# The MLP's down product as seven half-size block products, with the weights' block sums made by ScalarE and adding transfers

## The reference

```python
h2 = rms_norm(x, norm_mlp[layer])
x = x + jnp.square(jax.nn.relu(h2 @ w_ff1[layer])) @ w_ff2[layer]
return rms_norm(x, norm_final)
```

## Time and profile before

| | |
|---|---|
| Time, median of 3 runs | 1755.04 us (1754.81 to 1755.32) |
| The profiled execution's own time | 1756.95 us |
| Its span, first to last instruction | 1755.4 us |
| PE busy | 1741.1 us |
| DVE busy | 801.4 us |
| ACT busy | 587.6 us |
| POOL busy | 80.9 us |

### The profile page before, as it was taken

One profiled execution on the slowest core, in us unless ns is written; L12 is line 12 of the kernel. 1 busy time (PEld: TensorE's weight loads), 2 busy tenths in 40 slices (PEclk: granted clock), 3 DMA queues, 4 the chain that ended last, 5 costly groups with the idle time before them and its releaser, 6 DMA issues.

```text
span 1755.4 us, 21872 instructions
## 1 busy us (share of the span) xinstructions
PE 1741.1 (99%) x8476; PEld 1276.0 (73%) x8476; DVE 801.4 (46%) x1160; ACT 587.6 (33%) x753; POOL 80.9 (5%) x148
## 2 busy tenths in 40 slices
PE   8999999999999999999999999999999999999998
PEld 7888888874444444454788877788888888888886
DVE  6323338453242424333673455656675544324423
ACT  5334433332211212122454533444532253113313
POOL 3000000000000000000020022200000000000000
PEclk9999999999999999999999999999999999999999
DMA  6222222858999999999313221222242222222222
GB/s 207 94 97 94 72 72 97 340 213 347 422 422 422 422 421 422 422 422 413 109 50 125 96 89 56 73 97 96 96 173 99 101 96 96 96 96 96 96 97 82
DMA packets 91169, 326.34 MB, mean 186 GB/s; under 512 B 8720, under 2 KB 9248, under 8 KB 66528
## 3 DMA queue, kind: packets, MB, share of 16 engines
q1 hardware_dynamic: 89328, 320.18, 48.0%
q0 software_dynamic: 1776, 5.26, 0.9%
HBM read 319.13 MB, written 6.29 MB: 185 GB/s over the span
## 4 chain that ended last, share of the span: by engine, by line
PE 98%; DVE 1%; ACT 0%; DMA 0%; issue 0%; SPq 0%; DVEq 0%; ACTq 0%
PE bank L2321 62%; PE bank L2652 13%; PE bank L2665 6%; PE bank L2560 3%; PE bank L2607 3%; PE bank L2346 3%; PE bank L2894 2%; PE bank L2832 1%; PE bank L2776 1%; PE bank L2853 1%; PE bank L2534 0%; PE bank L2925 0%; PE bank L2523 0%; DMA w_stage<-in_w_in 0%; PE bank L2931 0%; PE bank L2910 0%
## 5 line engine op out<-in xcount | busy, mean ns | idle before, releaser
L2321 PE MATMUL bank<-act_hi,w_hi 128*128 128x512 f32 x992 | 389.7, 393 | 0.0
L2321 PE MATMUL bank<-act_hi,w_lo 128*128 128x512 f32 x992 | 386.3, 389 | 0.0
L2321 PE MATMUL bank<-act_lo,w_hi 128*128 128x512 f32 x992 | 386.2, 389 | 0.0
L1460 DVE TENSOR_TENSOR w_lo<-w_stage,w_hi 128x2048 fp32r<-128x2048 f32 x98 | 224.4, 2289 | 348.9 <-ACT w_hi L859 348.8
L859 ACT ACTIVATE w_hi<-w_stage 128x2048 fp32r<-128x2048 f32 x98 | 187.8, 1917 | 387.7 <-PE bank L2321 382.0
L2652 PE MATMUL bank<-ring,xgT 128*64 128x512 f32 x992 | 215.7, 592 | 0.2 <-ACT xgT L1078 0.2
L2321 PEld LDWEIGHTS bank<-act_hi,w_hi 128*128 128x128 f32 x992 | 186.3, 188 | 40.1 <-issue 2.5
L2321 PEld LDWEIGHTS bank<-act_hi,w_lo 128*128 128x128 f32 x992 | 186.2, 188 | 39.1
L2321 PEld LDWEIGHTS bank<-act_lo,w_hi 128*128 128x128 f32 x992 | 186.4, 188 | 37.5
L2652 PEld LDWEIGHTS bank<-ring,xgT 128*64 128x64 f32 x992 | 70.7, 137 | 141.5 <-issue 141.0
L2665 PE MATMUL bank<-ring,gatedT 128*64 128x512 f32 x512 | 113.4, 595 | 0.0
(11 more groups left out here) (429 smaller groups left out, 2036.1 us busy)
## 6 DMA issues: line engine op xcount, KB each, us to landing
ring<-in_w SPq DMA_DIRECT2D x188, 1024.0 KB, 12.0
w_stage<-in_w_in SPq DMA_DIRECT2D x45, 1024.0 KB, 5.1
w_stage<-in_w_ff SPq DMA_DIRECT2D x32, 1024.0 KB, 5.2
w_stage<-in_w_out SPq DMA_DIRECT2D x8, 1024.0 KB, 5.1
extra<-in_w SPq DMA_DIRECT2D x4, 1024.0 KB, 8.2
branch_gates<-gate_out POOLq DMA_DIRECT2D x16, 256.0 KB, 2.5
w_stage<-in_w_proj_gla SPq DMA_DIRECT2D x4, 1024.0 KB, 10.0
w_stage<-in_w_pg SPq DMA_DIRECT2D x3, 1024.0 KB, 5.1
```

The costliest lines, as they stand in the source:

```text
L1460: dve.tensor_tensor(w_lo[s][:, 0:ktiles, :], w_stage[s][:, 0:ktiles, :], w_hi[s][:, 0:ktiles, :].bitcast(F32), ALU.subtract).then_inc(w_lo ...
L2321: ins = pe.matmul(gb[j][:, :], left, right, start=(kc == 0 and k == 0 and n_pass == 0), stop=(kc == g.chunks - 1 and k == g.ktiles - 1 and ...
```

## The change

With the hidden tile as a 2 x 2 block matrix (token halves by hidden-feature halves, each block 256 x 1024) and the half's weights likewise (1024 x 512 blocks B11, B12, B21, B22), the eight block products of the down product become seven, each of one operand of the list `part_operand` with one weight operand: B11, B21, T2 = B22 - B12 + B11, T1 = B12 - B11, T3 = B22 - B12, B22, and B21 - T2. Part `n` has two steps `v = 2n, 2n+1`, each with one 1 MB weight operand, and serves 2 token tiles only: 24 matmuls a step. Parts that share a bank pair are left to add up in it (`part_first`), and each part is followed by an addition of its two banks to one quarter of `x` (`add_part`).

- `hid_hi`, `hid_lo` and `relu_sq` are gone. DVE squares straight into `hidden`, and each part's operand is split when its turn comes (`part_split_hi` on ACT, `part_split_lo` on DVE, 128x2048 each). `relu_t` has two buffers in place of four.
- The operands' sums are four DVE subtractions or additions of 128x2048 in each half (`sum_three`, `sum_two`, `sum_one`, `sum_four`).
- The weights' sums are made in SBUF: ACT negates a tile of 128x2048 (`negate`, eight in each half), and POOL then issues a DMA from `w_ff2` in DRAM with `accum_op=ALU.add` into that tile (`add_block`: in each half nine of 1 MB or, for `t3_late`, two of 512 KB in place of one, in one fixed order). Waits on POOL's queue keep the adds of one `kc` in order.
- The loops over the MLP's units on ACT and DVE are written out. The ends of the rows are taken in another order at the very end (token tiles 0 and 1 are done after part 5; tiles 2 and 3 after part 6). Elsewhere, three semaphores are merged with others, with the same waits.

```diff
-        last = Gemm(up, 2, FH // 512, "dve")
+        last = Gemm(up, 2, PARTS, "dve", tiles=PARTS)
...
-        hid_hi = at("hid_hi", F + 0, [P, FH // P, T], F32R)
-        hid_lo = at("hid_lo", F + 16, [P, FH // P, T], F32R)
-        relu_t = [at(f"relu_t{s}", F + 32 + s, [P, T]) for s in range(4)]
-        relu_sq = [at(f"relu_sq{s}", F + 36 + s, [P, T]) for s in range(4)]
+        hidden = at("hidden", F + 0, [P, FH // P, T])
+        a11, a12, a21, a22 = (hidden[:, 8 * i:8 * i + 8, 256 * q:256 * q + 256] for q in range(2) for i in range(2))
+        t3_late = a11.rearrange("p (k c) n -> p k c n", c=2)
+        part_hi = [at(f"part_hi{s}", F + 16 + 8 * s, [P, 8, 256], F32R) for s in range(2)]
+        part_lo = [at(f"part_lo{s}", F + 20 + 8 * s, [P, 8, 256], F32R) for s in range(2)]
+        b_one = [at(f"b_one{s}", F + 36 - 4 * s, [P, 4, 512]) for s in range(2)]
+        s_two = at("s_two", F + 36, [P, 8, 256])
+        b_sum = [at(f"b_sum{s}", F + 40 + 4 * s, [P, 4, 512]) for s in range(2)]
+        relu_t = [at(f"relu_t{s}", F + 48 + s, [P, T]) for s in range(2)]
...
+        part_bank = [(gb[0:2], mb[0:2], gb[0:2], gb[2:4], gb[0:2], gb[2:4], gb[0:2])[n] for n in range(PARTS)]
+        part_first = (True, True, False, True, False, False, False)
+        part_quarter = ((0, 0), (0, 0), (0, 1), (1, 1), (1, 1), (0, 1), (1, 0))
+        bank_before = (None, None, 0, None, 2, 3, 4)
+        S3, S2, S1, S4 = 1, 2, 3, 4
+        SUM_LOADS, STAGE_LOADS, ONE_LOADS, ADDS, NEGATED = 1, (2, 1), (3, 3), (5, 6), 8
+        step_stage = (w_stage[0], w_stage[1], w_stage[0], b_one[1], b_sum[0], b_sum[1], w_stage[0], w_stage[1],
+                      b_one[1], t3_late, b_one[1], b_one[0], b_sum[0], b_sum[1])
...
+        part_operand = (a11, a12, s_two[:, :, :], a11, a21, a12, a22)
...
-                load_units(up, A["w_ff1_2"][0], h * FH)
-                load_units(down, A["w_ff2_2"][0], 0, k0=h * FH // 512)
+                w_up = A["w_ff1_2"][0]
+                load_unit(up, 0, w_up, h * FH)
+                load_unit(up, 1, w_up, h * FH + 512)
+                if h == 0:
+                    sp.wait_ge(n_sd, rows_count(5, NT - 1))
+                    sp.wait_ge(n_lo, lows_before(5) + 2 * NT)
+                else:
+                    sp.wait_ge(w_lo_done, step(h - 1, 13))
+                for kc in range(2):
+                    sp.dma_start(b_sum[kc][:, :, :], weight_block(h, 0, 1, kc)).then_inc(b_sum_in[kc], 16)
+                load_unit(up, 2, w_up, h * FH + 2 * 512)
+                load_unit(up, 3, w_up, h * FH + 3 * 512)
+                sp.dma_start(b_one[1][:, :, :], weight_block(h, 1, 0, 1)).then_inc(b_one_in[1], 16)
+                for kc in range(2):
+                    sp.wait_ge(w_lo_done, split_count(up.chunk1 - 2 + kc))
+                    sp.dma_start(w_stage[kc][:, :, :], weight_block(h, 0, 0, kc)).then_inc(w_loaded[kc], 16)
+                sp.wait_ge(w_lo_done, step(h, 0))
+                sp.dma_start(w_stage[0][:, :, :], weight_block(h, 1, 0, 0)).then_inc(w_loaded[0], 16)
+                sp.wait_ge(w_lo_done, step(h, 3))
+                sp.dma_start(b_one[1][:, :, :], weight_block(h, 0, 1, 0)).then_inc(b_one_in[1], 16)
+                sp.wait_ge(part_low, PARTS * h + 4)
+                for c in range(2):
+                    sp.dma_start(t3_late[:, :, c, :], weight_block(h, 0, 1, 1)[:, :, c * 256:(c + 1) * 256])\
+                        .then_inc(b_one_in[0], 16)
+                sp.wait_ge(w_lo_done, step(h, 8))
+                sp.dma_start(b_one[1][:, :, :], weight_block(h, 1, 1, 0)).then_inc(b_one_in[1], 16)
+                sp.wait_ge(w_lo_done, step(h, 9))
+                sp.wait_ge(hid_summed, 4 * h + S4)
+                sp.dma_start(b_one[0][:, :, :], weight_block(h, 1, 1, 1)).then_inc(b_one_in[0], 16)
...
+            def add_block(h, kc, k, dst, block, beside=0):
+                pool.wait_ge(b_added[kc], loaded(h, "added", kc, k - 1 - beside))
+                pool.dma_start(dst, block, accum_op=ALU.add).then_inc(b_added[kc], 16)
+            for h in range(HALVES):
+                for kc in range(2):
+                    pool.wait_ge(b_negated, NEGATED * h + kc + 1)
+                    add_block(h, kc, 1, b_sum[kc][:, :, :], weight_block(h, 1, 1, kc))
+                for kc in range(2):
+                    add_block(h, kc, 2, b_sum[kc][:, :, :], weight_block(h, 0, 0, kc))
+                pool.wait_ge(b_negated, NEGATED * h + 3)
+                add_block(h, 1, 3, w_stage[1][:, :, :], weight_block(h, 1, 1, 1))
+                pool.wait_ge(b_negated, NEGATED * h + 4)
+                add_block(h, 0, 3, w_stage[0][:, :, :], weight_block(h, 1, 1, 0))
+                pool.wait_ge(b_negated, NEGATED * h + 5)
+                add_block(h, 0, 4, b_one[1][:, :, :], weight_block(h, 1, 1, 0))
+                pool.wait_ge(b_negated, NEGATED * h + 6)
+                add_block(h, 0, 5, b_sum[0][:, :, :], weight_block(h, 1, 0, 0))
+                pool.wait_ge(b_negated, NEGATED * h + 7)
+                for c in range(2):
+                    add_block(h, 1, 4 + c, t3_late[:, :, c, :], weight_block(h, 1, 1, 1)[:, :, c * 256:(c + 1) * 256],
+                              beside=c)
+                pool.wait_ge(b_negated, NEGATED * h + 8)
+                add_block(h, 1, 6, b_sum[1][:, :, :], weight_block(h, 1, 0, 1))
...
+            def part_split_hi(h, n):
+                if n >= 2:
+                    act.wait_ge(pe_tiles, 4 * (g_ff[h][1].chunk0 + 2 * n - 2))
+                elif h:
+                    act.wait_ge(pe_tiles, 4 * g_ff[h - 1][1].chunk1)
+                if n in (0, 1):
+                    act.wait_ge(hid_sq, hid_count(h, 2 * n + 2))
+                elif n < 6:
+                    act.wait_ge(hid_summed, 4 * h + {2: S2, 3: S1, 4: S3, 5: S4}[n])
+                act.activation(part_hi[n % 2][:, :, :], part_operand[n], ACT.Copy).then_inc(part_high, 1)
...
+            def step_split_hi(h, v):
+                down = g_ff[h][1]
+                done, buffers, k = {0: (w_loaded[0], "stage", 1), 1: (w_loaded[1], "stage", 1),
+                                    2: (w_loaded[0], "stage", 2), 3: (b_one_in[1], "one", 1),
+                                    4: (b_added[0], "added", 2), 5: (b_added[1], "added", 2),
+                                    6: (b_added[0], "added", 3), 7: (b_added[1], "added", 3),
+                                    8: (b_added[0], "added", 4), 9: (b_added[1], "added", 5),
+                                    10: (b_one_in[1], "one", 3), 11: (b_one_in[0], "one", 3),
+                                    12: (b_added[0], "added", 5), 13: (b_added[1], "added", 6)}[v]
+                slot = v % 2 if buffers == "added" else 0 if v == 11 else 1
+                act.wait_ge(done, loaded(h, buffers, slot, k))
+                act.wait_ge(pe_tiles, (down.chunk0 + v - 1) * 4)
+                act.activation(like(w_hi[v % 2], v), stage_of(v), ACT.Copy).then_inc(w_hi_done, 1)
...
+                    if u == 2:
+                        part_split_hi(h, 0)
+                    relu_unit(h, u)
+                    if u + 1 < up.units:
+                        split_hi(up.chunk0 + 2 * u + 3, 1)
+                    if u == 1:
+                        for kc in range(2):
+                            act.wait_ge(b_sum_in[kc], loaded(h, "sum", kc, 1))
+                            negate(b_sum[kc][:, :, :], b_sum[kc][:, :, :])
...
+                part_split_hi(h, 1)
+                step_split_hi(h, 2)
+                act.wait_ge(w_lo_done, step(h, 1))
+                act.wait_ge(b_added[1], loaded(h, "added", 1, 2))
+                negate(w_stage[1][:, :, :], b_sum[1][:, :, :])
+                for n in range(PARTS - 2):
+                    step_split_hi(h, 2 * n + 3)
+                    if n == 2:
+                        act.wait_ge(b_one_in[0], loaded(h, "one", 0, 2))
+                        negate(t3_late, t3_late)
+                    part_split_hi(h, n + 2)
+                    if n == 0:
+                        act.wait_ge(w_lo_done, step(h, 2))
+                        act.wait_ge(b_added[0], loaded(h, "added", 0, 2))
+                        negate(w_stage[0][:, :, :], b_sum[0][:, :, :])
+                    elif n == 1:
+                        act.wait_ge(b_one_in[1], loaded(h, "one", 1, 2))
+                        negate(b_one[1][:, :, :], b_one[1][:, :, :])
+                        act.wait_ge(w_lo_done, step(h, 4))
+                        negate(b_sum[0][:, :, :], b_sum[0][:, :, :])
+                    elif n == 2:
+                        act.wait_ge(w_lo_done, step(h, 5))
+                        negate(b_sum[1][:, :, :], b_sum[1][:, :, :])
+                    step_split_hi(h, 2 * n + 4)
+                if h + 1 < HALVES:
+                    step_split_hi(h, 13)
...
+            def add_part(h, n, j):
                 own.settle()
+                dve.wait_ge(pe_tiles, 4 * (g_ff[h][1].chunk0 + 2 * n + 1) + 2 * j + 2)
```

(80 more changed lines are left out.)

159 lines of the change are left out of this document (85 added, 74 removed).

## The result

The changed kernel takes 1759.11 us (median of 20 executions, 1756.29 to 1766.45), the kernel before 1755.24 us on the same chips (20 executions, 1754.80 to 1757.12). The ratio is 1.0022, with a 95% interval of 1.0014 to 1.0031: slower by 3.9 us, where I forecast 5 us faster. The profiled execution of the changed kernel took 1756.35 us, with a span of 1754.8.

A forecast was written before the change was run, and what follows sets the result against it. PE was taken to bound the kernel: -21.8 us for matmuls gone, +15.5 for holds in two halves, +1.2 at the end, -5.1 in all, so 1750 us (median 1749.9) against 1755.04; range 1737 to 1778 us.

The forecast's parts named there:

- What bounds the kernel, and what goes: MLP: only PE counts; the down product falls from 768 to 672 matmuls at 0.2267 us, saving 21.8 us.
- An add's price: POOL's 1 MB adding transfer: taken as twice a load, 5.0 us, between bounds of 2.5 and 7.5 us.
- My threshold of 5.5 us: Transfer time of an add at which the gain is gone; rival of slow adds, 1771 us at 7.5, chance 0.25.
- each us costs twice: Claim that each us more of an add's transfer costs twice at step 9 in each half; 1793 us at 9.5.
- the walk: Step-by-step account of PE's holds in a half of the down product: 1.07 + 2.1 + 4.6 = 7.8 us.
- step 9: Down product: t3_late's adds queue behind b_sum0's in POOL's order, landing at 30.3 us; PE holds 4.6 us in each half.
- Step 6: Down product: two negations on ACT stand before w_hi 6, so PE holds 1.07 us in each half.
- Step 8: Down product: t3_late's load shares the DMA engines with b_one1's add, delaying its negation and w_hi 8; PE holds 2.1 us.
- The clock: Rival: PE's clock falls to half in the hold at step 9, costing 5.4 us a half, 1761 us; chance 0.06.
- Step 11: Down product: no hold forecast, as all steps later than step 9 were to find their weights.
- The end: Kernel's end: last addition 8.3 us after w_lo 13, which comes 6.4 us before PE's end; 1.2 us more.
- Written-out loops, the sums of the operands, POOL's waits on DVE: Loops and sums: hidden, at no cost. Rival: DVE's two-input operations delay POOL's issues, 9 us in all, 1759; chance 0.04.

The follow-up runs named there:

- experiment 3: Changed kernel with POOL issuing t3_late's adds before b_sum0's, and ACT copying w_hi 6 and 8 ahead of the b_sum0 and b_sum1 negations: 1763.93 us.
- experiment 5: Changed kernel with b_one1's 1 MB add cut to 16 columns (8 KB), so step 8's weights lack a term: 1740.95 us, ratio 0.9916.
- experiment 9: Kernel of experiment 6, with b_one1's add waiting until t3_late's load has landed: 1743.93 us, ratio 0.9932.
- experiment 2: Changed kernel with POOL issuing t3_late's two adds before b_sum0's add: 1761.17 us, ratio 1.0030.
- experiment 4: Changed kernel with 20 extra matmuls into an unused bank ahead of part 4, to keep PE busy in step 8's hold: 1758.62 us, ratio 1.0022.
- experiment 8: Changed kernel with tiles of their own, loaded earlier, for the weights of steps 9, 10 and 11 in half 1: 1753.2 us, ratio 0.9994.
- experiment 11: Kernel of experiment 9 with ACT's w_hi 6 and 8 before the b_sum negations, and own early-loaded tiles for steps 8, 9, 11 in half 1: 1747.06 us.
- experiment 6: Changed kernel with t3_late's adds issued first and both b_sum adds last, after w_lo 9: 1751.73 us, ratio 0.9974.

## Why the prediction was wrong, point by point

- **What bounds the kernel, and what goes: right.** 672 matmuls at 0.2267 us when PE isn't held, so -21.8 us.
- **An add's price: right in kind, small in size.** I took 5.0 us of transfer; it is 5.7 (6.1 by the queue's share over the down product), 2.05 times a copy. My threshold of 5.5 us would have called the gain lost at this price. It doesn't follow from "each us costs twice", though: my own 7.8 us at 5.0 and 18.3 at 7.5 are 4.2 us of hold for each us, and at 9.5 my 28 us of holds would have been 1790, not 1793. With 5.7 put in, the walk gives 7.8 + 0.7 x 4.2 = 10.7 us a half, near the 10.4 measured. That would have been luck, since it puts the growth at step 9.
- **Step 6: right.** 0.94 us against 1.07, the queue on ACT (experiment 3 removes it).
- **Step 8: the step that failed.** "I let them share the DMA engines": by that `t3_late`'s load landed 4 us after PE left part 2, about 8.4 after its issue. It landed 11.3 us after its issue at 1514.17, at 6.9 us (1525.47, against ACT's start of `w_hi` 7 at 1518.58), and the hold was 5.0 us instead of 2.1, by the same 2.9. Experiments 5 and 9 show the cause: without the add beside it the load lands in at most 6.2 us, in experiment 9 with all the adds still made. I had made the load 3.2 us longer for sharing (8.4 instead of 5.2); the two transfers have 5.9 and 3.8 us of engine time, and the load landed with the add, at the end of both.
- **Step 9: landing nearly right, hold wrong.** The adds were to land 30.3 us after part 1's end and landed at 31.8 (1539.53 against 1507.70). But the hold of 4.6 us was mostly spent: 2.9 us more at step 8 and 2.9 of slow matmuls came first, and 0.24 us was left (1.8 in half 1, with fewer slow ones). In experiment 2 the lever I had named, POOL's order, gained nothing by itself.
- **The clock: the rival came true, one step earlier.** I had it at 0.06, after step 9, for 5.4 us a half. It fell after step 8's hold, for 14 matmuls, 2.9 us, and keeping it up gained nothing measurable, since the next wait took the time (experiment 4). TensorE: Matmul & The Clock Gate (section "Part 1: The HAM clock gate (the "warmup" mystery)") of the Trainium skill has the fall to half the clock after idleness; 0.43 us a matmul instead of 0.227 agrees.
- **Step 11: missed.** 0.86 us in half 0 and 0.65 in half 1, since the load of `b_one0` runs beside `b_sum1`'s add and takes 7.6 us. In sum the prediction had 7.8 us a half; the trace has 0.94 + 5.0 + 2.9 + 0.24 + 0.86 = 9.9 of the 10.4 in half 0, and most of the rest where the second matmul behind a wait starts 0.31 to 0.34 us after the first.
- **The end: mis-sized.** DVE's rows at the end:

```profile
1738.07 2.29 DVE L1662 TENSOR_TENSOR w_lo<-b_sum,w_hi 128x2048 fp32r<-128x2048 f32 x1 [1.75 <-ACT w_hi L1559]
1740.46 2.50 DVE L2511 TENSOR_TENSOR xn<-x_tm,gain 128x512 f32<-128x512 f32 x4
...
1748.70 0.75 DVE L2430 SCALAR_TENSOR_TENSOR x_tm<-bank,row_sums,x_tm 128x512 f32<-128x512 f32 x1
```

  From the end of `w_lo` 13 (1740.36) to the last addition it is 8.34 us, as forecast (8.3). But `w_lo` 13 comes 5.6 us before PE's end (1746.0), not 6.4: the squares of the last rows stand before `w_hi` 13 on ACT. PE's last matmul ends at 1746.16, so the addition is 2.5 us late, against 0.45 before: +2.1 us, not +1.2.
- **Written-out loops, the sums of the operands, POOL's waits on DVE: right at nothing,** as far as no wait of PE names them. POOL's issue of a 1 MB add takes 1.28 us, not the 0.54 of a store; in the changed kernel it lies on the chain once in a half, with 0.75 us.
- **The sum.** Measured terms: -21.8 + 2 x 10.4 + 2.1 = +1.1. I had set my 1750.3 against a span of 1755.4; most executions of the kernel before have spans of 1753.2 to 1753.8 (their time less about 1.6), so that base was 1.7 us long. The forecast of the time started from the median and isn't touched by it. 1753.7 + 1.1 = 1754.8, the profiled span after. The forecast of 1749.9 is missed by 9.2 us: 5.3 in the holds of the two halves, 0.9 at the end, 0.2 in the base (1755.24 instead of 1755.04), and 2.8 by which the median execution is longer than the profiled one. The longer ones tend to show lower mean clocks in their records (0.996 at 1756.3 us, 0.993 at 1760.3, 0.992 and 0.993 at 1764.6 to 1766.5); which step lengthens them stays open, since the profile is of a short one. One candidate is seen in another trace: in experiment 4, a long execution, a load of `w_proj_gla` before the MLP takes 17.4 us on the chain, and the first down product starts at 1491.0, where the other profiles have 1485.6 to 1487.8. Whether it acts in the change wasn't tested.

## What to carry to other kernels

When a change adds transfers to a stretch, sum all DMA time in it first, by the 10 us, and price a load that starts beside another transfer at the work of both. Here loads beside an add landed 2.4 us (step 11's, 7.6) to 6.6 us late (experiment 2, 11.8), against the 5.2 of the earlier trace rows, and moving transfers without keeping the urgent pair apart handed the wait to the next one (experiments 2, 3, 8, 11). A full stretch isn't lost by that: experiment 9 runs at 85% busy with 3.4 us of holds in half 0. What helped was to keep apart the two transfers whose results are due soonest, and to put off those that are due last (experiments 6 and 9: one wait and one moved add turned +3.9 us into -11.4). And a saving on the engine that bounds is a saving only if every feeder keeps to the shorter step. 22 us of matmuls were bought with 20 MB of adds, which take 20 x 5.7 = 114 us of the DMA engines.
